# First up projection of a three-layer chain: six output chunks computed from x times the norm's column factors, with the row factor and the shift applied at their eviction

## The reference

```
mixed = concatenate([h_a, h_b], axis=-1) @ w_out
x = x + ga1[:, None, :] * mixed
h = modulate(rms_norm(x, g_norm2), sh2, sc2)
x = x + ga2[:, None, :] * conv_glu(h, w_up, conv_w, conv_b, w_down)

rms_norm(x, g)    = x * rsqrt(mean(x*x) + EPS) * g
modulate(h, s, c) = h * (1 + c) + s
conv_glu: u, g = split(h @ w_up); g = 3-tap convolution of g over tokens; (gelu(g) * u) @ w_down
sh2, sc2, ga1, ... = columns of silu(c) @ w_ada + b_ada
```

## Time and profile before

| | us |
|---|---|
| device time, median of 3 runs | 2393.55 |
| lowest and highest of them | 2391.29, 2396.11 |
| span of the profiled execution (first to last instruction) | 2390.7 |
| TensorE busy in it | 2354.4 (98%), mean granted clock 0.991 |
| VectorE busy | 1870.1 (78%) |
| ScalarE busy | 1117.9 (47%) |
| chain that ended last, share of PE | 92% (DVE 4%, DMA 2%, ACT 1%, issue 1%) |

### The profile page before, as it was taken

How to read it: one execution, slowest core, us unless ns; L and a number is a source line. 1 busy time by engine, 2 the same in 40 slices (tenths; PEclk the granted TensorE clock), 3 DMA queues, 4 the chain that set the end, 5 groups by cost and what they waited for, 6 DMA issues and landing times.

```text
span 2390.7 us, 31739 instructions
## 1 busy us (share of the span) xinstructions
PE 2354.4 (98%) x13036; PEld 2030.2 (85%) x13036; DVE 1870.1 (78%) x2046; ACT 1117.9 (47%) x1383; POOL 5.3 (0%) x11
## 2 busy tenths in 40 slices
PE   6999999999999999999999999999999999999999
PEld 3688888888888888888888888898888888889987
DVE  6889888898888678888778878778787667685754
ACT  2153445545554434555445445634555334455552
POOL 0000000000000000000000000000000000000000
PEclk8799999999999999999999999999999999999999
DMA  9999776695777688777775898766777773764343
GB/s 396 360 337 353 282 282 238 229 333 210 271 273 271 216 273 295 270 273 272 244 241 182 332 327 315 272 239 236 264 264 272 273 281 138 259 226 159 124 160 140
DMA packets 119009, 620.24 MB, mean 259 GB/s; under 512 B 13392, under 2 KB 14672, under 8 KB 76112
## 3 DMA queue, kind: packets, MB, share of 16 engines
q1 hardware_dynamic: 70560, 446.45, 52.5%
q10 hardware_dynamic: 48304, 171.76, 19.5%
HBM read 616.06 MB, written 2.10 MB: 259 GB/s over the span
## 4 chain that ended last, share of the span: by engine, by line
PE 92%; DVE 4%; DMA 2%; ACT 1%; issue 1%; SPq 0%; POOL 0%; DVEq 0%; POOLq 0%; ACTq 0%
PE pm L603 26%; PE ps L603 14%; PE pm L604 13%; PE ps L604 7%; PE pm L642 5%; PE pm L644 5%; PE pm L643 5%; PE ps L644 2%; PE ps L642 2%; PE ps L643 2%; DVE acc_first L1688 2%; DMA e<-in_ada 1%; DMA ada<-in_ada 1%; PE px L928 1%; DVE w_lo L1626 1%; PE px L815 1%
## 5 line engine op out<-in xcount | busy, mean ns | idle before, releaser
L1626 DVE TENSOR_TENSOR w_lo<-raw,w_hi 128x2048 fp32r<-128x2048 f32 (+2 forms) x412 | 892.3, 2166 | 354.4 <-ACT w_hi L1141 352.8
L1141 ACT ACTIVATE w_hi<-raw 128x2048 fp32r<-128x2048 f32 (+2 forms) x412 | 747.5, 1815 | 548.4 <-DMA raw<-in_w_down 119.3
L603 PE MATMUL pm<-h,w_hi 128*128 128x512 f32 x2318 | 798.8, 391 | 0.4 <-DVE ka L1677 0.2
L604 PE MATMUL pm<-h,w_lo 128*128 128x256 f32 x2318 | 640.9, 276 | 0.0
L603 PEld LDWEIGHTS pm<-h,w_hi 128*128 128x128 f32 x2318 | 435.2, 188 | 93.6 <-issue 2.2
L604 PEld LDWEIGHTS pm<-h,w_lo 128*128 128x128 f32 x2318 | 435.3, 188 | 0.2
L603 PE MATMUL ps<-h,w_hi 128*128 128x512 f32 x1186 | 410.6, 391 | 0.8 <-DVE w_lo L1626 0.8
L1638 DVE SCALAR_TENSOR_TENSOR acc<-ada,csil,acc 128x1024 f32<-128x1024 f32 x300 | 383.9, 1280 | 1.5
L604 PE MATMUL ps<-h,w_lo 128*128 128x256 f32 x1186 | 328.1, 277 | 0.0
L603 PEld LDWEIGHTS ps<-h,w_hi 128*128 128x128 f32 x1186 | 222.7, 188 | 48.8 <-issue 2.0
L604 PEld LDWEIGHTS ps<-h,w_lo 128*128 128x128 f32 x1186 | 222.7, 188 | 0.1
(11 more groups left out here) (434 smaller groups left out, 2979.5 us busy)
## 6 DMA issues: line engine op xcount, KB each, us to landing
ada<-in_ada ACTq DMA_DIRECT2D x320, 512.0 KB, 5.5
raw<-in_w_up SPq DMA_DIRECT2D x88, 1024.0 KB, 5.0
raw<-in_w_in SPq DMA_DIRECT2D x56, 1024.0 KB, 6.2
raw<-in_w_down SPq DMA_DIRECT2D x64, 704.0 KB, 5.0
raw<-in_sgu_v SPq DMA_DIRECT2D x32, 1024.0 KB, 5.0
raw<-in_sgu_u SPq DMA_DIRECT2D x32, 1024.0 KB, 5.4
raw<-in_sgu_z SPq DMA_DIRECT2D x32, 1024.0 KB, 5.0
raw<-in_sgu_out SPq DMA_DIRECT2D x32, 1024.0 KB, 4.9
```

The source lines that it names most:

```text
L603: pe.matmul(dst[:, :], wh[:, k, :], hl, start=(kc == 0), stop=False, skip_group_check=True)
L604: mm = pe.matmul(dst[:, 0:T], wl[:, k, :], hi, start=False, stop=last, skip_group_check=True)
L1141: act.activation(hi_(q, n), raw_(q, n), ACT.Copy).then_inc(hi_ready, 1)
L1626: tt_(lo_(q, n), raw_(q, n), whole(hi_(q, n)), ALU.subtract).then_inc(lo_ready, 1)
```

## The change

For the first six columns of `w_up0`, PE no longer multiplies h but a new operand, `rough_up` = x * a in high and low halves, with two more columns per chunk that hold the high and low half of the shift s. It needs no row factor, so it is made during `w_out`: three chunks in each of the columns 11 to 15, the last chunk after the residual. A tile now takes three matmuls: `w_hi` on 258 columns (high half and both shift columns), `w_hi` on 256 (low half), `w_lo` on 258. All go to the same 258 PSUM columns. At the eviction DVE multiplies by `rstd` and adds the two shift columns up (`early_scale`), and ACT adds that sum as a bias (`early_shift`). PE sums the squares within the first column, after nine tiles; the 12 matmuls without a reader are gone; `fold_group(1)` stands after column 9 of `w_out`. The real h is still needed from column 6 on; it is made in parts of three or four chunks between the evictions of columns 0 to 4 (`UP_PARTS`). The pieces of the modulation are moved: 7 out of `w_out` into `vb` and `oa`, and those of `w_up0` start at its column 6 instead of 0. Some tiles of the MLP stage have new places in SBUF.

```diff
-ADA_SPANS = [..., ("vb", 0, 14, 17), ("w_out", 0, 13, 19),
-             ("w_up0", 0, 40, 32), ...
+ADA_SPANS = [..., ("vb", 0, 15, 24), ("w_out", 0, 9, 12),
+             ("w_up0", 6, 37, 32), ...
...
+RW = 2 * T + LINE
+ROUGH_AT = {11: range(0, 3), 12: range(3, 6), 13: range(6, 9), 14: range(9, 12), 15: range(12, 15)}
+UP_PARTS = {0: range(0, 3), 1: range(3, 6), 2: range(6, 9), 3: range(9, 12), 4: range(12, 16)}
...
 # PE
+            def early_tile(stage, c, kc):
...
+                pe.matmul(dst[:, 0:T + 2], wh[:, kc, :], r[:, kc, T:2 * T + 2], start=(kc == 0), stop=False, ...)
+                pe.matmul(dst[:, 0:T], wh[:, kc, :], r[:, kc, 0:T], start=False, stop=False, ...)
+                mm = pe.matmul(dst[:, 0:T + 2], wl[:, kc, :], r[:, kc, T:2 * T + 2], start=False, stop=(kc == KC - 1), ...)
...
-            fold_group(1)
-            sum_squares([("norm2", 0)])
-            keep_running(NORM_STEPS["norm2"])
+                if c == 9:
+                    fold_group(1)
...
+                    for c in range(EARLY[up]):
+                        for kc in range(KC):
+                            if c == 0:
+                                rough_needed(up, kc)
+                            if (c, kc) == (0, 9):
+                                sum_squares([("norm2", 0)])
+                            early_tile(up, c, kc)
+                    for c in range(EARLY[up], COLUMNS[up][0]):
+                        columns(up, c, both(h), (lambda g: h_needed("norm2")(4 * g + 3)) if c == EARLY[up] else None)
...
 # ACT
+                act.activation(rough[norm][:, kc, T:2 * T], x[:, kc, :], ACT.Identity, scale=gain[:, k, kc:kc + 1])...
+                act.activation(dst, dst, ACT.Identity, bias=early_bias[:, c:c + 1]).then_inc(half_out, 1)
...
 # DVE
+                stt(r[:, kc, 0:T], x[:, kc, :], gain[:, k, kc:kc + 1], whole(r[:, kc, T:2 * T]), ALU.mult, ALU.subtract)...
+            def early_scale(stage, c, dst):
+
+                dve.wait_ge(piece_done, done(stage, c))
+                tt_(dst, bank(stage, c)[:, 0:T], rstd[:, :], ALU.mult)
+                dve.tensor_reduce(early_bias[:, c:c + 1], bank(stage, c)[:, T:T + 2], AX.X, ALU.add).then_inc(...)
...
+                    if 2 * i < EARLY.get(up, 0):
+                        if i == 0:
+                            rsqrt_mean("norm2", D)
+                        early_scale(up, 2 * i, gpad[:, k % 2, 1:1 + T])
+                        normed_part("norm2", SH2, UP_PARTS.get(2 * i, ()))
+                    else:
+                        second_half(up, 2 * i, gpad[:, k % 2, 1:1 + T])
                     begin(up, 2 * i + 1)
                     if i:
                         glu_low(k - 1)
+                    if 2 * i < EARLY.get(up, 0):
+                        normed_part("norm2", SH2, UP_PARTS.get(2 * i + 1, ()))
```

More of the change, by code:

```diff
@@ L232, in build @@
         rstd = sb("rstd", [P, T])
+        early_bias = sb("early_bias", [P, 8])
         o_ssq = cursor[0]
@@ L315, in build @@
              [at_(f"pt{j}", [P, 384], o_nt + 384 * (j - 2)) for j in (2, 3)]
+        rough = {"norm2": work("rough_up", [P, KC, RW], 7168, F32R)}
         pm = [ctx.enter_context(nc.psum_tensor(f"pm{b}", [P, 512], F32)) for b in range(2)]
@@ L606, in columns, with rough_needed @@
                     mm.then_inc(piece_done, 1)
+            def early_tile(stage, c, kc):
+                n, q, r = UBASE[stage] + c, piece(stage, c), rough[EARLY_OF[stage]]
+                dst = ring[n % 3]
+                if kc == 0:
+                    if n >= 3:
+                        pe.wait_ge(bank_free[n % 3], n // 3)
+                    pe.wait_ge(lo_ready, q + 1)
+                wh, wl = (halves(w(q, PIECE), KC) for w in (hi_, lo_))
+                pe.matmul(dst[:, 0:T + 2], wh[:, kc, :], r[:, kc, T:2 * T + 2], start=(kc == 0), stop=False, skip_group_check=True)
+                pe.matmul(dst[:, 0:T], wh[:, kc, :], r[:, kc, 0:T], start=False, stop=False, skip_group_check=True)
+                mm = pe.matmul(dst[:, 0:T + 2], wl[:, kc, :], r[:, kc, T:2 * T + 2], start=False, stop=(kc == KC - 1), skip_group_check=True)
+                if kc == KC - 1:
+                    mm.then_inc(piece_done, 1)
+            def rough_needed(stage, kc):
+                pe.wait_ge(rough_ready, rough_count(EARLY_OF[stage], kc))
             def column_pair(stage, src, need):
@@ L1176, in last_square, with rough_shift, rough_high, early_shift @@
                 act.activation(sqt[:, j, :], x[:, KC - 2 + j, :], ACT.Square).then_inc(sq_ready, 1)
+            def rough_shift(norm, group, shift):
+                act.wait_ge(fold_taken, group + 1)
+                act.wait_ge(gain_set, ROUGH.index(norm) + 1)
+                act.activation(rough[norm][:, :, 2 * T], mods[:, shift * KC:(shift + 1) * KC], ACT.Copy).then_inc(rough_hi, 1)
+            def rough_high(norm, kc):
+                k = H_NORMS.index(norm)
+                act.activation(rough[norm][:, kc, T:2 * T], x[:, kc, :], ACT.Identity, scale=gain[:, k, kc:kc + 1]).then_inc(rough_hi, 1)
+            def early_shift(stage, c, dst):
+                summed(stage, c)
+                act.activation(dst, dst, ACT.Identity, bias=early_bias[:, c:c + 1]).then_inc(half_out, 1)
+                act.wait_ge(half_out, halved(stage, c))
             def root(name):
@@ L1348, in _ @@
                     pair_squares("w_out", "norm2", c // 2 - 1, x_pair(c // 2 - 1))
+                if c in ROUGH_AT:
+                    if c == min(ROUGH_AT):
+                        rough_shift("norm2", 1, SH2)
+                    summed("w_out", ROUGH_AT[c][-1])
+                    for kc in ROUGH_AT[c]:
+                        rough_high("norm2", kc)
             summed("w_out", KC - 2)
             last_square("norm2", 0)
-            split(piece(*GAP_SPLITS["norm2"]))
             summed("w_out", KC - 1)
+            rough_high("norm2", KC - 1)
             last_square("norm2", 1)
-            root("norm2")
-            modulate("norm2", SH2)
             def gated_unit(up, i, k):
```

90 lines of the change are left out of this document (69 added, 21 removed).

## The result

The changed kernel takes 2405.40 us (median of 8 runs, 2402.82 to 2416.13), the kernel before 2394.83 us beside it (8 runs, 2391.29 to 2400.14). The ratio is 1.0043, 95% interval 1.0026 to 1.006: slower by some 10 us, where 1.4 us of gain had been forecast and 2398 was the upper end of the range. The profiled execution took 2410.11 us, with a span of 2408.3; in every run listed here the device time lies some 1.8 us above the span.

The account below looks back on a forecast made before the run. PE was taken to set the pace before the seam, with DVE having nothing to spare, then ACT and DVE turns to delay columns 6 and 7. -3.3 + 1.9 = -1.4 on 2393.55 gave 2392.2 us, range 2387 to 2398.

Parts of the forecast that it names:

- The seam and the tiles: From w_out into w_up0: the seam closes, three-matmul tiles take 0.36 us, sums of squares 1.8 us.
- the term of 3.3 us gained: Seam and first columns of w_up0: column 7 starts at 45.4 instead of 49.5, less 0.8 for the fold.
- weight loads: Rival, new w_up0 tiles: each matmul held to its weight load, 0.57 us per tile, +15 us, 2409 us; chance 0.05.
- open seam: Rival, start of w_up0: late rough_up stops PE in column 0, nothing gained, 1.9 lost, 2395.5 us; chance 0.02.
- The turns of ACT and DVE: Columns 0 to 7 of w_up0: alternating splits and h parts start column 6 at 37.7, column 7 at 45.4; waits 3.6 us.
- the sums: First column of w_up0: eight records of the sum of squares on PE, 1.8 us.
- The full gain: Rival, w_up0: no piece late and unit's end hidden in oa, 6.9 us gained, 2386.7 us; chance 0.15.
- The moved pieces: vb and oa: six of seven pieces fit; PE waits 1.9 us for s_b near 441, bounds 0 and 2.5.
- The head waves: Rival, vb and oa: seven pieces and the unit's end come on PE's path, +8.4 us, 2402 us; chance 0.08.
- The sum of these: Whole kernel: -3.3 at seam and turns, +1.9 for moved pieces, -1.4 us.
- The 2.85 us between the profiled execution and the median: Offset used to turn the profiled execution's forecast span of 2389.3 into the median forecast of 2392.2 us.

Follow-up runs that it names:

- flat_best: flat_end with 23 pieces in vb and oa, and ACT splitting before adding shifts in w_up0: seven runs at 2386.2 to 2388.5 us, five at 2392.4 to 2395.3.
- before_64: Kernel before plus one unused tile of 8 words behind rstd, so ssq, sqt, nt and the work area lie 64 bytes higher: ratio 1.0057.
- before_moved: Kernel before with only the changed kernel's placement (early_bias allocated but unused; gpad, conv, uu at new offsets), old instructions: no time given, loss present.
- again_after: The changed kernel, unchanged, run and profiled a second time: median 2408.99 us.
- flat_end: Changed kernel with early_bias at the end of SBUF and 24 pieces of vb and oa over 16 columns, not 15: stretch 415.4 us, no total given.
- flat_turns: flat_end with parts of h laid around the splits in columns 0 to 4 of w_up0: stretch 418.1 us, no total given.
- again_before: The kernel before, unchanged, run and profiled a second time: 12 runs at 2390.8 to 2404.6 us.
- before_roll: Kernel before plus one unread 128x256 matmul behind columns 3, 7, ... 39 of w_up0 and w_up1: single execution, no total given.
- before_glu: Kernel before with only glu and gpad 64 bytes higher: w_down0 and w_down1 +2.2 and +2.4 us, no total given.

## Why the prediction was wrong

- **The seam and the tiles: right.** 0.36 a tile, no unread matmuls, 1.5 us for the sums (1.8 forecast); the term of 3.3 us gained is 415.3 + 1.8 - 413.6 = 3.5 by the stretches (413.6 is the mean of the four kernels with the changed order). The rivals on weight loads and on the open seam are out.
- **The turns of ACT and DVE: right.** Columns 6 and 7 start within 0.2 us of the forecast, and flat_best shows the cause. The turns cost more than the 3.6 forecast, 45.6 - 41.4 = 4.2, and column 5 waited too (0.3); the sums, sized too high, made up for it. The full gain was to be had with another order of the same instructions; my rival had treated it as a matter of durations.
- **The moved pieces: right.** 1.9 forecast; 1.62 of wait, 1.8 in the stretch. The head waves did not overflow elsewhere.
- **The sum of these: right.** -1.4 forecast, 413.6 - 415.3 = -1.7 measured.
- **One comparison that cost nothing.** The 2.85 us between the profiled execution and the median set a span against a device time. Some 1.8 of them lie between the two in every run. They cancel in the forecast.
- **The failed step is one that I left out.** In the prediction the sum ended with "-3.3 + 1.9 = -1.4", and everything outside these places was carried over at the durations of before. The diff put `early_bias` in front of the work area, which raised every tile behind it by 64 bytes, among them `glu`, `y` and `hx`, which PE reads in `w_down0` and `w_down1`, `sgu_out` and `w_out`. The tiles of the projections that slowed down read what didn't move; why they did is open. By before_64 and before_moved against before that costs 1.6 in proj, 0.7 in `w_out`, 2.1 and 2.2 in `w_down0` and `w_down1` and 4.6 to 4.9 in `sgu_out`, 11.3 in all. The prediction had these terms at nothing. -1.7 + 11.3 = +9.6; the ratio of 1.0043 says +10.3 on 2394.83, that of again_after +13.
- **The range was too narrow for another reason too.** Each of `w_up0` and `w_up1` can be 6 us longer in one execution of a kernel than in another. The profiled run of before had neither, that of after had one. Taken alone, that pair of profiles would have put 5.5 us down to the change that come and go with the execution.

## What to carry to other kernels

A diff has two parts, its instructions and its addresses. Where tiles are laid out one behind the other, look at what a new small one pushes, and put it at the end. And when two profiles are compared, first look whether the unchanged stages still keep their pace (matmuls per window); only what is left is the change's. A wait of TensorE has to be priced with what its clock does behind it: in flat_end and flat_turns 3.4 us of waiting cost another 1.7 and 2.7. An order in which two engines hand over to each other can cost as much as the work: here 4 us came back by splitting first and adding afterwards.

## What the hardware showed

- The spacing of back-to-back matmuls at a granted clock of 1.00 changes with the place of their operands in SBUF. For `glu`: 0.340 us per tile at the old place, 0.347 at 64 bytes higher (five profiles), 0.350 at 128 higher (one), 0.353 in `w_down0` with also the weights' high half 64 higher (one). Why, no run shows. The Trainium skill ("TensorE: Matmul & The Clock Gate", section "Back-to-back issue gap") gives N / 2.4 + 2.5 ns as the gap of an isolated matmul and says that for large N in a stream this is too much. As an estimate by that page the two matmuls of a tile would take 0.325 us. None of the four spacings is that, all are above it, and the traces decide.
- The place isn't all. Tiles of h in proj, at unchanged places, went from 0.340 to 0.350 when the tiles of the matmuls ahead of them, and of ACT and DVE beside them, lay 64 bytes higher (before_64).
- At unchanged places a stage on h runs at 0.340 or, from its first columns to its end, at 0.350. `w_up1` did so in 6 of the 15 profiles without unread matmuls in it, `w_up0` in 2. Of four unread matmuls that fell into slow tiles (before_roll) two were followed by 0.340. What begins such a run of slow tiles stays open: in again_before the one in `w_up1` stands behind a pause of 1.02 us, in before_glu there is no pause there, and pauses of 0.37 and 0.73 us at the same place in before_64 and before_moved were followed by 0.340.
- Behind waits of 3.4 us the granted clock was 0.50 (flat_end from 462.2 to 465.4, flat_turns from 597.2 to 602.8) and then 1.00 again; behind waits of 1.09 and 1.72 us it stayed at 1.00 (after, from 590.5 and from 598.5).
